# Expert rows gated before the down product and scatter-added into the residual rows in memory; the tail reads eight summed tiles

## What is computed

```python
gates = (g_gate * top_v / jnp.sum(top_v, -1, keepdims=True)).reshape(-1)   # two per token
...
def expert_block(args):                      # a block of up to 128 rows with one expert e
    xb, e = args
    hid = jax.nn.silu(xb @ w_gate[e]) * (xb @ w_up[e])
    return hid @ w_down[e]
...
out = segment_sum(ys * row_gate[:, None], row_tok)        # the token's two rows, gated and summed
h = h + out                                               # residual; the next norm reads h
```

## Time and profile before

| | |
|---|---|
| median of 3 runs | 2790.54 us (2790.24 to 2793.55) |
| the profiled execution | 2791.1 us, its span 2789.3 us |
| granted PE clock over the span | 0.963 of full speed |
| busy: PE, DVE, ACT, POOL | 2574.3, 1913.4, 1608.3, 378.0 us |
| memory read, written | 506.06 MB, 50.33 MB |
| scatters of expert rows (L1438) | 64, that is 32 in each layer |
| loads of expert rows (L1386) | 32 of 512 KB, 16 in each layer |

### The profile page before, as it was taken

How to read it: one execution, slowest core, us unless ns; L and a number is a source line. 1 busy time by engine, 2 the same in 40 slices (tenths; PEclk the granted TensorE clock), 3 DMA queues, 4 the chain that set the end, 5 groups by cost and what they waited for, 6 DMA issues and landing times. The chain is left out here.

```text
span 2789.3 us, 58868 instructions
## 1 busy us (share of the span) xinstructions
PE 2574.3 (92%) x21332; PEld 2077.8 (74%) x21332; DVE 1913.4 (69%) x2191; ACT 1608.3 (58%) x1874; POOL 378.0 (14%) x342
## 2 busy tenths in 40 slices
PE   6998899988979999999969999998797999999995
PEld 5776799946758888888748777776684888888882
DVE  5348356534469999999655676677436899999973
ACT  3656223243338888888635566556222788888872
POOL 0020000000003333333201000000000222222220
PEclk9999999988989999999979999999898999999997
DMA  4111000013259999999641111111324999999974
GB/s 114 38 38 31 27 4 4 4 62 116 102 182 368 379 384 383 381 374 380 239 192 31 39 37 35 39 32 47 123 76 156 362 377 380 383 382 383 380 275 194
DMA packets 219995, 525.45 MB, mean 188 GB/s; under 512 B 43824, under 2 KB 99120, under 8 KB 219824
## 3 DMA queue, kind: packets, MB, share of 16 engines
q1 hardware_dynamic: 201392, 489.34, 47.5%
q0 software_dynamic: 18432, 33.60, 3.2%
HBM read 506.06 MB, written 50.33 MB: 199 GB/s over the span
## 5 line engine op out<-in xcount | busy, mean ns | idle before, releaser
L1812 DVE TENSOR_TENSOR w_low<-w_raw,w_high 128x1024 fp32r<-128x1024 f32 x768 | 894.9, 1219 | 31.7 <-DVEq L52 22.0
L1490 ACT CAST w_high<-w_raw 128x1024 fp32r<-128x1024 f32 x768 | 755.4, 1049 | 109.7 <-ACTq L52 108.8
L1665 PE MATMUL ps<-w_high,x_high 128*128 128x512 f32 x1024 | 414.9, 405 | 7.0 <-PEq L52 6.1
L1669 PE MATMUL ps<-w_high,x_low 128*128 128x512 f32 x1024 | 403.9, 394 | 0.0
L1668 PE MATMUL ps<-w_low,x_high 128*128 128x512 f32 x1024 | 401.9, 392 | 0.0
L1665 PEld LDWEIGHTS ps<-w_high,x_high 128*128 128x128 f32 x1024 | 195.4, 191 | 50.3 <-issue 13.6
L1669 PEld LDWEIGHTS ps<-w_high,x_low 128*128 128x128 f32 x1024 | 194.1, 190 | 43.4
L1668 PEld LDWEIGHTS ps<-w_low,x_high 128*128 128x128 f32 x1024 | 194.9, 190 | 37.6
L1665 PE MATMUL ps<-w_high,hidden_high 128*128 128x512 f32 x512 | 200.9, 392 | 6.7 <-PEq L52 6.7
L1668 PE MATMUL ps<-w_low,hidden_high 128*128 128x512 f32 x512 | 200.4, 392 | 0.0
L1669 PE MATMUL ps<-w_high,hidden_low 128*128 128x512 f32 x512 | 200.4, 391 | 0.0
(11 more groups left out here) (428 smaller groups left out, 4941.2 us busy)
## 6 DMA issues: line engine op xcount, KB each, us to landing
w_raw<-in_moe_w_gate SPq DMA_DIRECT2D x256, 512.0 KB, 5.4
w_raw<-in_moe_w_up SPq DMA_DIRECT2D x256, 512.0 KB, 5.7
w_raw<-in_moe_w_down SPq DMA_DIRECT2D x256, 512.0 KB
w_raw<-expert_rows SPq DMA_DIRECT2D x32, 512.0 KB, 9.3
w_tiles<-in_c_w_in SPq DMA_DIRECT2D x28, 512.0 KB, 4.0
w_tiles<-in_ab_w_in SPq DMA_DIRECT2D x22, 512.0 KB, 3.8
residual<-in_x SPq DMA_DIRECT2D x16, 512.0 KB, 7.6
h_rows<-hn_moe SPq DMA_DIRECT2D x16, 512.0 KB, 2.9
```

What stands on the lines that cost most here:

```text
L1490: act.copy(wh[:, p, :], raw[:, p, :]).then_inc(high_made, 1)
L1665: ins = pe.matmul(ps[:, bank, :], high, w_h, start=first, stop=False)
L1669: return pe.matmul(ps[:, bank, :], low, w_h, start=False, stop=final)
L1812: dve.tensor_tensor(wl[:, p, :], raw[:, p, :], wh[:, p, :].bitcast(F32), ALU.subtract).then_inc(low_made, 1)
```

## The change

After the change

- the gate of each row is laid out in the order of the blocks (`gate_row`): DVE multiplies the one-hot tile by the gates (one instruction of 768 elements a partition), PE runs 16 more small matmuls, plain float32, between the 16 that build the place table and the last seven of `stay_warm`, and DVE copies the result once, ahead of its first step;
- `hidden` becomes a `scalar_tensor_tensor` that multiplies the gate in, with the row's gate column addressed by the loop's index;
- SP stores each residual tile to `residual_rows` in the front, right behind the store of `h_rows`; POOL waits for these stores before its first gather;
- the scatter goes to `residual_rows` by token and adds to what lies there;
- the tail loads the eight residual tiles from memory in one piece each; `sum_rows`, `combine`, the row scales, the place table's copy, and layer 0's store of the residual at the end are gone. The eight loads wait for nothing but `y_all`.

```diff
-        scales, mixed = sem("scales"), sem("mixed")
+        gates_spread, gates_placed = sem("gates_spread"), sem("gates_placed")
...
-        lay([f32("x_rows", D)], [f32("row_scale", TT, P)])
-        xg, scale_by = at["x_rows"], at["row_scale"]
+        xg = sb("x_rows", [P, D])[:]
+        gate_row = sb("gate_of_row", [P, NBLK])
...
+        at_gate = at["sel_rank"].rearrange("p a e t -> p (a e t)")[:, 0:2 * TT * NBLK].rearrange("p (i b) -> p i b", b=NBLK)
...
                     sp.dma_start(c.rows[t * P:(t + 1) * P, :], hn[:, t % 2, :]).then_inc(rows_in[t % 2], 16)
+
+                    sp.dma_start(c.res_rows[t * P:(t + 1) * P, :], c.res[:, t, :]).then_inc(kept, 16)
...
                 sp.wait_ge(y_all, 1)
-                for i in range(2 * TT):
-                    t, k = i // 2, i % 2
-                    if i >= NPC:
-                        sp.wait_ge(used, i - NPC + 1)
-                    sp.dma_start(raw[:, i % NPC, :], c.ys[k * S + t * P:k * S + (t + 1) * P, :]).then_inc(raw_in[i % NPC], 16)
-                    if i == 1:
+                for t in range(TT):
+                    sp.dma_start(c.res[:, t, :], c.res_rows[t * P:(t + 1) * P, :]).then_inc(raw_in[t], 16)
+                    if t == 1:
                         sp.dma_start(gb2, next_gain.partition_broadcast(P)).then_inc(next_in, 16)
...
+                pool.wait_ge(kept, 16 * TT)
...
-                    pool.tensor_copy(idx[:, 1:2], dst_row[:, b]).then_inc(order_p, 1)
+                    pool.tensor_copy(idx[:, 1:2], src_tok[:, b]).then_inc(order_p, 1)
                     take(pool, order_p)
-                    pool.indirect_dma_start(c.ys, bass.IndirectOffsetOnAxis(ap=idx[:, 1:2], axis=0), yb, None,
-                                            bounds_check=2 * S - 1, oob_is_err=False).then_inc(arrival, 16)
+                    pool.indirect_dma_start(c.res_rows, bass.IndirectOffsetOnAxis(ap=idx[:, 1:2], axis=0), yb, None,
+                                            bounds_check=S - 1, oob_is_err=False, compute_op=ALU.add).then_inc(arrival, 16)
...
                 def next_square(t):
-                    act.wait_ge(combined, t + 1)
+                    take(act, raw_in[t], 16)
...
-                def sum_rows(t):
...
                 last.then_inc(placed, 1)
+                pe.wait_ge(gates_spread, 1)
+                for i in range(2 * TT):
+                    last = pe.matmul(ps[:, B_S, 0:NBLK], at_pos[:, i, :].bitcast(F32), at_gate[:, i, :], start=i == 0, stop=i == 2 * TT - 1)
+                last.then_inc(gates_placed, 1)
                 stay_warm(7)
...
-                    dve.tensor_tensor(hid, hid, ps[:, B_U, :], ALU.mult).then_inc(hid_ready, 1)
+                    dve.scalar_tensor_tensor(out=hid, in0=hid, scalar=gate_row[:, b], in1=ps[:, B_U, :], op0=ALU.mult,
+                                             op1=ALU.mult).then_inc(hid_ready, 1)
...
                 ch(dve.tensor_tensor(gate[:, 1, :], gate[:, 0, :], col["m2"], ALU.mult))
+                dve.tensor_tensor(at_gate, reach[:, :, 0:NBLK], bcast(gate[:].rearrange("p k t -> p (k t)"), 2, NBLK), ALU.mult).then_inc(gates_spread, 1)
...
-                ch(dve.tensor_copy(dst_row[:], dstf))
...
-                step(0)
-                with dve.Fori(1, n):
-                    step(1)
-                    step(0)
-                step(1, last=True)
-                def combine(t):
...
+                dve.wait_ge(gates_placed, 1)
+                ch(dve.tensor_copy(gate_row[:], ps[:, B_S, 0:NBLK]))
+                step(0, slice(0, 1))
+                with dve.Fori(1, n) as i:
+                    step(1, bass.ds(2 * i - 1, 1))
+                    step(0, bass.ds(2 * i, 1))
+                step(1, bass.ds(2 * n - 1, 1), last=True)
...
-                combine(0)
+                next_mean(0)
                 dve.wait_ge(next_in, 16)
-                combine(1)
-                next_mean(0)
                 for t in range(TT):
                     next_rows(t)
-                    if t + 2 < TT:
-                        combine(t + 2)
```

More of the change, by code:

```diff
@@ L1262, in moe @@
              f32("prod", TT, EPG, NG), *(f32(n, TT, EPG) for n in ("e_logits", "e_rest", "e_hot1", "e_hot2")),
-             f32("sel", 2, NE, TT), f32("rank_sel", 2, NE, TT),
+             f32("sel_rank", 4, NE, TT),
              *(f32(n, NE, TT) for n in ("sel_both", "counts", "rank", "far")), f32("cmp_blocks", NE, EPG),
@@ L1299, in moe @@
         prod, ex, ex2, oh1, oh2 = (at[n] for n in ("prod", "e_logits", "e_rest", "e_hot1", "e_hot2"))
-        sel, both, incl, rank, far, rsel = (at[n] for n in ("sel", "sel_both", "counts", "rank", "far", "rank_sel"))
+        both, incl, rank, far = (at[n] for n in ("sel_both", "counts", "rank", "far"))
+        sel, rsel = at["sel_rank"][:, 0:2], at["sel_rank"][:, 2:4]
+        at_gate = at["sel_rank"].rearrange("p a e t -> p (a e t)")[:, 0:2 * TT * NBLK].rearrange("p (i b) -> p i b", b=NBLK)
         cmp8, nblk, over, oend, jump = (at[n] for n in ("cmp_blocks", "n_blocks", "over", "over_end", "jump"))
@@ L1381, in _ @@
                 sp.wait_ge(y_all, 1)
-                for i in range(2 * TT):
-                    t, k = i // 2, i % 2
-                    if i >= NPC:
-                        sp.wait_ge(used, i - NPC + 1)
-                    sp.dma_start(raw[:, i % NPC, :], c.ys[k * S + t * P:k * S + (t + 1) * P, :]).then_inc(raw_in[i % NPC], 16)
-                    if i == 1:
+                for t in range(TT):
+                    sp.dma_start(c.res[:, t, :], c.res_rows[t * P:(t + 1) * P, :]).then_inc(raw_in[t], 16)
+                    if t == 1:
                         sp.dma_start(gb2, next_gain.partition_broadcast(P)).then_inc(next_in, 16)
-                for t in range(TT):
-                    if last_norm:
+                if last_norm:
+                    for t in range(TT):
                         sp.wait_ge(next_ready, t + 1)
                         sp.dma_start(out[t * P:(t + 1) * P, :], hn2[:, t % NB, :]).then_inc(rows_in[t % 2], 16)
[L1393 to L1396, removed]
                     for q in range(2):
                         sp.wait_ge(rows_in[q], 16 * TT)
-                else:
-                    sp.wait_ge(kept, 16 * TT)
             @block.gpsimd
@@ L1620, in next_turn @@
                     last.then_inc(next_turned, 1)
-                def sum_rows(t):
[L1623 to L1631, removed]
-                    last.then_inc(mixed, 1)
                 def turn_rows(t):
@@ L1752, in first_head @@
                     first_projection(pe, c, m, 0, h_high, h_low).then_inc(c.first_done, 1)
-                if last_norm:
+                if not last_norm:
                     for t in range(TT):
-                        sum_rows(t)
-                else:
-                    sum_rows(0)
-                    sum_rows(1)
-                    for t in range(TT):
-                        if t + 2 < summed_tiles:
-                            sum_rows(t + 2)
                         next_turn(t)
@@ L1827, in hidden_low, with step @@
                                       hh.rearrange("p k n -> p (k n)").bitcast(F32), ALU.subtract).then_inc(hl_ready, 1)
-                def step(q, last=False):
+                def step(q, b, last=False):
                     if not last:
@@ L1833, in step @@
                         low(range(2, 2 * GU))
-                    hidden()
+                    hidden(b)
                     low(down_p)
@@ L1931, in _ @@
                 x_low(0)
-                step(0)
-                with dve.Fori(1, n):
-                    step(1)
-                    step(0)
-                step(1, last=True)
-                def combine(t):
-                    if t < summed_tiles:
-                        i, b = 2 * t + 1, sum_bank(t)
-                        take(dve, raw_in[i % NPC], 16)
-                        dve.wait_ge(mixed, t + 1)
-                        dve.scalar_tensor_tensor(out=c.res[:, t, :], in0=raw[:, i % NPC, :], scalar=gate[:, 1, t:t + 1],
-                                                 in1=ps[:, b:b + 2, :].rearrange("p b n -> p (b n)"), op0=ALU.mult, op1=ALU.add).then_inc(used, 2)
-                        dve.wait_ge(used, 2 * t + 2)
-                        dve.sem_inc(combined, 1)
-                        return
-                    for k in range(2):
-                        i = 2 * t + k
-                        take(dve, raw_in[i % NPC], 16)
-                        if k:
-                            dve.wait_ge(used, i)
-                        last = dve.scalar_tensor_tensor(out=c.res[:, t, :], in0=raw[:, i % NPC, :], scalar=gate[:, k, t:t + 1],
-                                                        in1=c.res[:, t, :], op0=ALU.mult, op1=ALU.add)
-                        last.then_inc(used, 1)
-                    dve.wait_ge(used, 2 * t + 2)
-                    dve.sem_inc(combined, 1)
```

(3 more changed lines are left out.)

8 lines of the change are left out of this document (2 added, 6 removed).

## The result

The changed kernel takes **2795.4 us** (median of 12 runs, 2790.8 to 2798.2) against 2790.1 for the kernel before on the same chip: a ratio of 1.0023, 95% interval 1.0015 to 1.0031. So it is slower, by little: the interval lies clear of 1. Forecast were 2755 and a range of 2744 to 2785.

A forecast was written before the change was run, and what follows sets the result against it. PE was taken to bound the loop, busy 395.65 of 395.97 us. Tails -22.4 and -20, last scatters +3, router +3.5, loop terms 0 gave -35.9 against 2791.1; forecast 2755 us, range 2744 to 2785.

The forecast's parts named there:

- the adding scatter in the loop: Block loop: adding rows cost 0.70 us more a block, need 17.0 under 17.92, so hidden, 0 us.
- the share of 0.99: Block loop: profiled DMA engine share at 381 GB/s; if true, need is 17.74 + 0.70 = 18.44 us a block.
- rival B: Block loop becomes the DMA engines': 18.44 us a block, +14 us, total 2769; chance 0.13.
- The lead: Block loop: weight loads land 9.6 us before ACT takes the tile, time to spare before PE waits.
- Rival D: Loop: adding rows hold their DMA engine for read, then write; slower than before, 2883 at 0.8 us more a row; chance 0.14.
- Both signs: Prediction is wrong if the loop's block grows, or the last scatter takes several us more than 3.35.
- Layer 1's tail: End of layer 1: last row scaling at 2756.7 instead of 2779.06, tiles 1.82 us apart, -22.4 us.
- Layer 0's tail: End of layer 0: tiles 2.9 us apart, PE's remaining 23.2 us stay, -20 us.
- The last scatter: Before each tail's loads: now reads before writing, +1.5 us each, +3 us for two; bounds nothing and +3.35.
- The router: Before each layer's first block: DVE work and 16 float32 matmuls on PE, about +3.5 us for two layers; ends -2 and +12.
- `hidden` in the loop: Block loop, DVE: gate multiplied in, +0.07 us each against 0.12 to spare, so 0 us.

The follow-up runs named there:

- the first run with a load more: Kernel before plus one plain load a block, 64 rows of 4 KB from the gathered rows' memory over the last residual tile: 2903.0 us, ratio 1.0408.

## Why the prediction was wrong

**The step that failed** is the adding scatter in the loop: "At 418 GB/s the present 6.83 MB need 16.3 us, so 17.0, still under 17.92: hidden, 0 us." Two parts of it:

- The second half, one more 0.70 us a block, held: +0.73 by the queues. The Trainium skill (Collectives: The Full Stack, The bandwidth ceiling) says of the adding step of a collective that it reads two sources and so runs at half the rate of a copy. The trace agrees with the rate, 327 ns a row against 159; that the second read is the cause, no row shows.
- The first half did not: the need of 17.84 us before is what the share of 0.99 said, not 16.3. 418 GB/s came from four microseconds of a tail with plain 512 KB loads and no scatter or gather. It was the wrong row for a loop whose own row stood beside it. Not that the share is exact: plain bytes of the same size raised the rate to 394 GB/s and cost 6 to 8 us in all, less than their packets' time. The time of the adding rows found no such room.

So rival B came true, and its size was off as well. It had 18.44 us a block; it is 18.75 of need, by 0.10 (17.84 for 17.74), 0.03 (0.73 for 0.70) and 0.19, the weights' packets that got slower beside the adding rows, for which I had no term. Measured over PE's 17.93, a block of 18.83 is 0.90 more, and not 0.52. The lead was sized fairly: 31 blocks from first to last gather would have cost 27.9 us and did cost 564.7 - 545.1 = 19.6 in layer 1, so 8.3 us of it were covered, against 9.6; the gate loads' landing, 7.9 us later than before, says much the same. As the loss is what is left after the lead, 0.38 us a block more and 1.3 us less of lead became 13 us a layer more than in rival B. Rival D's point, growth of 0.86 us a block eating the whole gain, was just passed, and its side of the result came true, but not by its size of a row: from a need of 17.74 it wanted 260 ns more a row, and a row takes 327 - 159 = 168 ns more. The rest came from the need, 17.84 and not 17.74, and from the weights. Both signs that the prediction named for its being wrong came: the block grew, and the last scatter took 3 us more.

**The other steps.**

- Layer 1's tail, -22.4: the first row scaling came 7.8 us after the loads (7.94 worked out) and the last 21.7 after them, against 43.0: -21.4. Right within 1 us. The second tile was 2.97 behind the first, the others 1.82.
- Layer 0's tail, -20: 7.7 us from the loads to the first row scaling, and 45.4 from the loads at 1419.74 to the stage's end at 1465.18, against 65.2 before: -19.7. Right.
- The last scatter, +1.5 each: 6.6 us and 6.1 until the loads against 3.35, so +3.3 and +2.8. This is the upper bound I had given; without the adding it is 3.3 again. The added time is about that of a whole second trip, not of a part of one.
- The router, +3.5 for two layers: first transposes 8.8 and 9.5 us behind the first gather against 5.0 and 5.8 before, +3.8 and +3.7. But the first block then runs faster, and up to the first scatter it is +2.2 and -0.2. The 16 float32 matmuls took the upper bound:

```profile
783.76 7.06 PE L1718 MATMUL ps<-sel_rank_moe,at_pos_moe 128*128 128x48 f32 x32 [1.04 <-DVE sel_rank_moe L1897]
790.62 7.42 PE L1701 MATMUL ps<-residual,ones 128*128 128x512 f32 x14
797.88 1.11 PE L1636 MATMUL ps<-ident,x_rows 128*128 128x128 f32 x8
```

- `hidden` in the loop, 0: it takes 0.74 us for 0.68, and the loop without adding is as fast as before. Right.

The sum without the adding was good: 2755 less the 3 us for the last scatters is 2752, and 2754.5 was measured with the adding left out. That 2755 and 2754.5 agree so closely is luck.

## What to carry to other kernels

When a loop's row shows PE at 100% and the DMA engines at 0.99, both are close to the bound. What is put on the DMA engines next first uses up the prefetch lead and then lengthens the block: here by all of the adding rows' time (0.90 us, where the need gave 0.82) and by a part of the plain bytes' (0.2 to 0.4, where it gave 0.55). Take the need of a block from that loop's own queue shares (share times block time), never from the peak rate of a quieter stretch, and look at how landing times grow along the loop before calling a stretch with a busy PE free. An adding scatter trades a load and a sum in the tail for twice the engine time of every scattered row in the loop, so it pays only where the loop has DMA time to spare. And look at the order of small instructions in a tail before moving its work elsewhere: here two swaps, root before square and variance before the next sum, gave 4 to 10 us by the interval in the kernel before.

## What the hardware showed that I had not expected

- A load of 0.26 MB a block as 4 KB to each of 64 partitions cost 112 to 114 us in all, where the same bytes as 2 KB to each of 128 cost 8: it raised the mean of all 4 KB packets of the weights' queue from 170 to 182 ns. Why such a load slows the others, where a store from 64 partitions (+6 us) does not, was not tried.
- The DMA share of a stretch can pass 1.00 (1.01 at 391 to 394 GB/s), and shares of 0.97 to 1.01 went with anything from 346 to 394 GB/s.
- On POOL the adding scatter's own instruction takes longer than the plain one, 1571 to 3436 ns against 976 to 2844 in layer 0. The medians, 1607 and 2841, say the opposite, but both kinds vary from block to block: in layer 1 of the kernel before the plain one's median is 1842, and in layer 0 of the first run with a load more it is 1020. The shortest landing is 6.5 us against 3.2.
